# Weight pieces of 1 MB in eighteen ring places, logits without a wait for the last turned tile, and two small moves beside the first pair, in a two-layer MoE decoder trunk

## What is computed

```python
def reference(x, ...):
    h = x
    for i in range(2):
        xn = rms_norm(h, norm_mix[i])
        mix = sliding_window_attention(xn, ...) if i == 0 else gated_short_conv(xn, ...)
        h = h + mix
        h = h + hierarchical_moe(rms_norm(h, norm_ffn[i]), ...)
    return rms_norm(h, final_norm)

def hierarchical_moe(h, w_group, b_group, w_expert, b_expert, w_gate_up, w_down):
    group_probs = softmax(xt @ w_group + b_group)          # 4 groups, top 1
    exp_logits = xt @ w_expert + b_expert                  # 8 experts in a group, top 2
    ...
    def expert_block(xb, e):                               # 32 experts
        g, u = split(xb @ w_gate_up[e], 2)                 # w_gate_up[e]: 1024 x 1024
        return (silu(g) * u) @ w_down[e]                   # w_down[e]: 512 x 1024
```

## Time and profile before

| | us |
|---|---|
| three runs | 1341.44, 1341.86, 1343.41 |
| median | 1341.86 |
| the profiled execution's own time | 1341.31 |
| its span | 1339.6 |

### The profile page before, as it was taken

The page is one execution under the profiler, slowest core; times in us unless marked ns, Lnnn a source line. Parts: engine busy times, 40 slices in busy tenths (PEclk is TensorE's granted clock), DMA queues, the critical chain, the costliest instruction groups (busy, mean ns, idle before and its releaser), DMA issues.

```text
span 1339.6 us, 15996 instructions
## 1 busy us (share of the span) xinstructions
PE 1281.9 (96%) x6188; PEld 687.6 (51%) x6188; DVE 498.7 (37%) x1178; ACT 311.7 (23%) x622; POOL 148.9 (11%) x122
## 2 busy tenths in 40 slices
PE   7999999999999998989999999999999999999896
PEld 5777664444444433334588888744444444433342
DVE  5586342223222322224656662432223222322235
ACT  3267611111111111111443321211111111111103
POOL 4950120000000000000000002200001000000000
PEclk9999989999999999999999999899999999999999
DMA  9901569999999999999823336689999999999997
GB/s 347 342 8 60 255 259 419 429 427 428 429 427 429 428 428 426 428 427 426 257 88 105 103 142 267 250 347 427 427 428 428 427 428 428 429 426 428 426 428 296
DMA packets 68579, 462.53 MB, mean 345 GB/s; under 512 B 18020, under 2 KB 33406, under 8 KB 43956
## 3 DMA queue, kind: packets, MB, share of 16 engines
q1 hardware_dynamic: 63232, 452.87, 81.6%
q0 software_dynamic: 4800, 7.96, 1.6%
q10 hardware_dynamic: 500, 1.06, 0.2%
HBM read 443.40 MB, written 26.24 MB: 351 GB/s over the span
## 4 chain that ended last, share of the span: by engine, by line
PE 75%; DMA 21%; DVE 2%; ACT 0%; issue 0%; SPq 0%; POOLq 0%; DVEq 0%
PE ps L1170 22%; PE ps L962 20%; PE ps L1188 13%; DMA big<-in_moe_w_gate_up_dram 12%; PE ps L1145 8%; DMA small<-in_moe_w_gate_up_dram 6%; DMA big<-rows 2%; PE ps L1160 2%; PE ps L1179 1%; PE ps L926 1%; PE ps L1105 1%; PE ps L1271 1%; PE ps L1154 1%; PE ps L1044 1%; PE ps L1011 1%; PE ps L945 1%
## 5 line engine op out<-in xcount | busy, mean ns | idle before, releaser
L1170 PE MATMUL ps<-big,arena 128*64 128x512 f32 x976 | 218.2, 594 | 17.1 <-DMA big<-in_moe_w_gate_up_dram 15.6
L1685 DVE SCALAR_TENSOR_TENSOR gain<-ps,slot_root,arena 64x512 f32<-64x512 f32 x64 | 72.8, 1137 | 403.1 <-ACT arena L810 402.1
L617 POOL DMA_INDIRECT rows<-arena x60 | 59.0, 983 | 827.7 <-DVE arena L1713 827.7
L1170 PEld LDWEIGHTS ps<-big,arena 128*64 128x64 f32 x976 | 68.9, 137 | 158.4 <-issue 131.1
L810 ACT ACTIVATE arena<-ps,slot_root 64x512 f32<-64x512 f32 x64 | 43.7, 682 | 452.6 <-PE ps L1170 452.6
L1170 PE MATMUL ps<-small,arena 128*64 128x512 f32 x496 | 111.9, 593 | 5.1 <-DMA small<-in_moe_w_gate_up_dram 5.1
L962 PE MATMUL ps<-xt_parts,small_parts 128*128 128x512 f32 x288 | 110.6, 393 | 0.0
L962 PE MATMUL ps<-xr_parts,small_parts 128*128 128x512 f32 x272 | 105.9, 389 | 0.0
L1188 PE MATMUL ps<-big,arena 128*64 128x512 f32 x432 | 98.7, 598 | 1.5 <-DMA big<-in_moe_w_down_dram 1.5
L962 PE MATMUL ps<-xt_parts,big_parts 128*128 128x512 f32 x256 | 99.7, 389 | 0.0
L1170 PEld LDWEIGHTS ps<-small,arena 128*64 128x64 f32 x496 | 35.4, 137 | 77.0 <-issue 68.3
(11 more groups left out here) (218 smaller groups left out, 1687.7 us busy)
## 6 DMA issues: line engine op xcount, KB each, us to landing
big<-in_moe_w_gate_up_dram SPq DMA_DIRECT2D x61, 2048.0 KB, 27.9
small<-in_moe_w_gate_up_dram SPq DMA_DIRECT2D x31, 2048.0 KB, 28.6
big<-in_moe_w_down_dram SPq DMA_DIRECT2D x27, 2048.0 KB, 30.1
arena<-in_moe_w_gate_up_dram SPq DMA_DIRECT2D x16, 2048.0 KB, 30.1
small<-in_moe_w_down_dram SPq DMA_DIRECT2D x11, 2048.0 KB, 28.7
xt<-in_moe_w_gate_up_dram SPq DMA_DIRECT2D x10, 2048.0 KB, 25.4
h<-in_moe_w_gate_up_dram SPq DMA_DIRECT2D x10, 2048.0 KB, 24.7
xt<-in_moe_w_down_dram SPq DMA_DIRECT2D x10, 2048.0 KB, 31.8
```

Source lines behind the costliest of these rows:

```text
L617: nc.gpsimd.indirect_dma_start(out=rows_dram[l], out_offset=bass.IndirectOffsetOnAxis(ap=where[:, j:j + 1], axis=0), in_=S.y_rows[:, j, :] ...
L1170: mm = nc.tensor.matmul(ps[2 + j][half * BLOCK:(half + 1) * BLOCK, :], S.xg[:, k, j * BLOCK:(j + 1) * BLOCK], w[:, a, half * FF:(half + 1) ...
L1685: V.scalar_tensor_tensor(out=hid[BLOCK:P, j, :].rearrange("q (k p) -> q p k", p=P), in0=ps[2 + j][BLOCK:P, :].rearrange("q (p k) -> q p k" ...
```

## The change

Five edits:

1. A pair has twelve pieces of 1 MB (`PIECES = 12`, `PIECE = 2` rows to a partition), and the ring eighteen places, the halves of the old nine. The order of the bytes is the same. `gu_done` now counts quarters of a `w_gate_up`, `down_done` halves of a `w_down`. A run in HBM is 8 KB where it was 16 KB.
2. The semaphores of four loads of `x` and five others of the first stage are those of ring places 9 to 17, which are used later; the counts take this in.
3. `turn_tile` of the last tile ends without the wait for all copies in the two stages that come before logits; `logits` waits for its own tile alone.
4. For the first pair ACT copies one half of the gathered rows and DVE the other.
5. `last_gates` follows the first `take` and `find_rows`.

```diff
-    PIECES = 6
-    RING = 9
+    PIECES = 12
+    PIECE = 2
+    RING = 18
...
-        x_in = [sem(f"x_in{t}") for t in range(TT)]
...
+        FIRST_IN = RING // 2
+        x_in = ring_in[FIRST_IN:FIRST_IN + TT]
+        rel_in, query_in, w_o_in, kv_in, bo_in = ring_in[FIRST_IN + TT:]
...
+        ring = [[place[:, at:at + PIECE] for place in of_layer for at in range(0, FT, PIECE)] for of_layer in places]
...
                             before, used = divmod(n - RING, PIECES)
-                            if used < 4:
-                                sp.wait_ge(main[l].gu_done, 4 * before + used + 1)
+                            if used < 8:
+                                sp.wait_ge(main[l].gu_done, 8 * before + used + 1)
...
-                        if c < 4:
-                            w = w_gate_up[l, 2 * i + c // 2].rearrange("(p k) n -> p k n", p=P)[:, c % 2 * FT:(c % 2 + 1) * FT]
+                        if c < 8:
+                            w, part = w_gate_up[l, 2 * i + c // 4], c % 4
                         else:
-                            w = w_down[l, 2 * i + c - 4].rearrange("(p k) n -> p k n", p=P)
+                            w, part = w_down[l, 2 * i + (c - 8) // 2], c % 2
+                        w = w.rearrange("(p k) n -> p k n", p=P)[:, part * PIECE:(part + 1) * PIECE]
                         sp.dma_start(ring[l][n % RING], w).then_inc(ring_in[n % RING], 16)
...
             def experts(l):
                 S = main[l]
-                take_picked(S, 0)
+                take_picked(S, 0, (0,))
...
                     keep_busy(busy, 5)
+                    if i in (1, 3):
+                        return
                     pe.wait_ge(xt_even, TT * (i + 1))
                     pe.wait_ge(xt_odd, TT * (i + 1))
...
             def gate_up(S, j, part, w):
-                for a in range(FT):
-                    k = part * FT + a
+                for a in range(PIECE):
+                    k = part * PIECE + a
...
-            def down(S, n, j, w):
-                pe.wait_ge(S.hidT_ready, n + 1)
-                for k in range(FT):
+            def down(S, n, j, part, w):
+                if part == 0:
+                    pe.wait_ge(S.hidT_ready, n + 1)
+                for a in range(PIECE):
+                    k = part * PIECE + a
...
                 select(main[l], slice(0, 2))
+                dve.wait_ge(main[l].gathered, 1)
+                V.tensor_copy(picked[:, HALF:D], ps[1][:]).then_inc(main[l].rows_taken, 1)
                 dve.wait_ge(rank_ps, 2 * l + 2)
...
                 layer_gain[0] = gffn[:, l]
-                last_gates()
                 if l == 0:
                     dve.wait_ge(scales_in, 32)
                     dve.wait_ge(cleared, 16 * L)
                 take(S, 0)
                 find_rows(S, 0)
+                last_gates()
```

More of the change, by code:

```diff
@@ L536, in _ @@
                 if q < BIG_SLOTS:
[L537 removed]
+                    sp.wait_ge(main[0].gu_done, 4 * E)
                 else:
@@ L797, in router, with take_picked @@
                 nc.scalar.activation(rt[:, :, 20:21], rt[:, :, 20:21], ACT.Exp).then_inc(exp_ready, 1)
-            def take_picked(S, i):
+            def take_picked(S, i, halves_taken=(0, 1)):
                 act.wait_ge(S.gathered, i * 3 + 1)
-                for half in range(2):
+                for half in halves_taken:
                     nc.scalar.activation(picked[:, half * HALF:(half + 1) * HALF], ps[half][:], ACT.Copy)\
```

61 lines of the change are left out of this document (29 added, 32 removed).

## The result

The changed kernel takes 1349.08 us (median of 5 runs, 1348.28 to 1349.92) beside 1341.44 us of the kernel before in the same comparison: a ratio of 1.0057, 95% interval 1.0042 to 1.0072. It is 7.6 us slower. The forecast was 1346.6 us with a range of 1334 to 1350.5; case A came about, 2.5 us above its middle.

The account below looks back on a forecast made before the run. The prediction took the full transfer engines, streaming expert weights, as the bound. From the profiled 1341.31 us, -5.6 (moment) - 0.5 (tail) + 10.9 (rate) gave 1346.1, or 1346.6 for the median of runs; range 1334 to 1350.5.

Parts of the forecast that it names:

- case A: Weight stream: 8 KB packets have the rate of the line through other packet sizes; 1346.6 us, 1342.6 to 1351, chance 42%.
- The form of the sum: Each layer's experts: the moment the stream becomes continuous, plus bytes still to come over the rate, plus a fixed tail.
- (a): First expert matmuls: a ring place is free after half a piece, so the next load issues 1.75 us earlier per layer.
- (b): First pair's take: with last_gates behind it, DVE takes the first half sooner, 0.45 us a layer, 0.9 in all.
- (c): First pair's row copy on two engines: nothing gained, since PE's own order starts the turning.
- (d): Logits before the experts: matmuls start 0.65 and 0.9 us earlier, gaining 0.5 us in layer 0 and 0.7 in layer 1.
- its upper bound: Logits term: if the clock should not fall, or rise sooner, DVE's masks set the start, 1.8 us in each layer.
- the moment: Tenth load's issue, when the stream becomes continuous: 5.6 us earlier over both layers, between 4.2 and 8.0.
- The empty stretch takes all of it: Empty queue before the tenth load, 6 us in each layer: long enough to absorb the whole earlier moment.
- The rate: Expert weight stream: 8 KB packets go at 422.6 GB/s, 5.4 us later per layer, 10.9 in all.
- rival B: Weight stream: 16 KB rate is a ceiling 8 KB packets also reach, so only gains stand; 1335.8 us, chance 33%.
- The tail: Layer 0's end: PE may get to some of line 1247's matmuls sooner, 2 us at most; 0.5 us gain taken.

Follow-up runs that it names:

- half pieces alone: The changed kernel with the three small edits (logits, two-engine copy, last_gates) undone, keeping 1 MB pieces in eighteen places: 1352.49 us, ratio 1.0098 to the kernel before.
- the kernel of two loads: The kernel before with each 2 MB piece fetched by two 1 MB loads of 8 KB runs into the same nine places: 1351.31 us, ratio 1.0087.
- a single half place: Kernel before plus the three small edits, whole pieces, only each layer's tenth piece fetched as two 1 MB loads: 1335.12 us, ratio 0.9970 to the kernel before.
- the small edits: The kernel before with only the logits, two-engine copy and last_gates edits, pieces whole: 1335.24 us, ratio 0.9972; again 1335.75 us, 0.9976.
- the three kernels above: The kernel before with gate and up in 8 KB runs (ratio 1.0078), all pieces in 8 KB runs (1.0113), or gate and up in 4 KB runs (1.0182).

## Why the prediction was right, and where its sizes were not

**The form of the sum** held: a moment, plus the stream, plus a tail. The stream was full to the end, PE waited for the half pieces near the end, as it had for the whole ones, and the rows followed the weights. PE in layer 0, pair 14, where the earlier trace rows has pieces 4.92 us apart (these lines are from the changed kernel's timeline):

```profile
598.38 1.94 PE L1174 MATMUL ps<-big,arena 128*64 128x512 f32 x8 [0.35 <-DMA big<-in_moe_w_gate_up_dram]
600.87 1.94 PE L1174 MATMUL ps<-small,arena 128*64 128x512 f32 x8 [0.56 <-DMA small<-in_moe_w_gate_up_dram]
```

Half pieces come 2.5 us apart.

**(a) Half pieces, -1.75 a layer.** Measured -1.72 and -1.71 from the first matmuls to the issue. Against the kernel with 8 KB runs and whole places, though, issue to rows is 0.3 (half pieces alone) to 0.6 us (the changed kernel) longer, so 1.1 to 1.4 net, and less against the kernel of two loads. Not seen in the prediction; with a single half place 0.7 to 0.9 are left.

The prediction covered twice the loads with 0.33 us for each issue. That held for the first pairs, but not later: from 440 to 636 us 63 of 73 issues of a load of 1 MB take over 1.5 us, 2.1 in the middle and up to 6.6. Four of them in the changed kernel:

```profile
598.05 11.13 SPq L482 DMA_DIRECT2D big<-in_moe_w_gate_up_dram  x4
```

The kernel before has 0.33 us for each there, and so have the small edits; every kernel whose stream has 8 or 4 KB packets has long ones, with a median over the weight loads of that stretch of 2.1 us for 1 MB and of 4.6 to 5.2 us for 2 MB. Could this, and not the packet, be what slows the stream? No: in the changed kernel the stream has the same rate ahead of it, 421 GB/s with 0.33 us for every issue from 240 to 290 us, and in it, 421 from 440 to 600.

```profile
240.00:290.00 50.00, 50.00 (x249) 20.65 (x246) 13.54 (x34) 7.94 (x13) 3.89 (x4) 1.00 1.01 421
440.00:600.00 160.00, 148.02 (x700) 59.16 (x696) 37.47 (x87) 23.18 (x36) 10.27 (x11) 1.00 1.01 421
```

**(b), (c) Takes and gates, -0.45 and 0.** Measured 0.3 to 0.4 for both together in each layer.

**(d) Logits, -0.5 and -0.7.** At equal clock right in layer 0 (0.6) and short in layer 1 (1.1); beside the one profile of before mis-sized. In layer 1 the clock did not fall at all, so the stretch from turning to selection lost 3.2 us (13.28 to 10.12), of which 1.1 is the edit's. In layer 0 it lost 2.3 us (13.18 to 10.90), of which 0.6 is the edit's and the rest a shorter fall. The prediction had this as its upper bound ("If the clock should not fall, or rise sooner", 1.8 in each layer), with DVE's masks taking over as the limit, and that is the row at 864.77, waiting 1.16 for DVE. The step that failed was to move the matmuls under a clock that stays where one profile had it: whether and for how long it falls differs from one profile to the next. In all the moment came 9.5 us sooner, not 5.6, and 3.8 of the 9.5 are this difference between two profiles; at equal clock it is 5.7.

**"The empty stretch takes all of it"** held, and just. In layer 1 the moment came 5.2 us sooner, and of the 6 us next to nothing is left: the traffic there runs on at 422 and 299 GB/s. Any further gain ahead of the experts would find about one microsecond to fill in layer 1 and 2 us in layer 0.

**The rate, +5.4 a layer.** Mis-sized: +7.1 and +7.4. Two causes. The larger is the cost of a packet: the prediction laid one line through the 4 KB row (6 ns a packet) and one through the 1 KB row (9 ns) and took the middle. The kernel with the same packets in whole places lost 6.5 and 6.9 us, 9.3 and 9.9 ns for each of the 696, so the line through 1 KB was the better one and 421.5 GB/s the rate, not 422.6. The rest, 0.6 and 0.5, is what the half pieces lose in the stream, under (a).

A fixed part for each packet beside one for the bytes is what the three kernels above show: 428 GB/s with 16 KB, 421.5 with 8 KB, 1.5% less, and 409 with 4 KB, which is worked out above. So 428 GB/s is no ceiling that packets of 16 and 8 KB both reach, as rival B had it. Take 9 ns off the 612.5 ns of a 16 KB packet, and its bytes alone would go at 434 GB/s, an estimate from these two numbers.

**The tail, -0.5.** Wrong in sign: +2.07 at the end of layer 0. PE does end its last down product sooner, by 1.7 us against the first row tile. But the step that failed was what PE's 2.33 us of idle time were put down to: the prediction had PE wait for DVE's rest, so that 12 of the 32 matmuls could go ahead of it. PE was in its branch until 646.40, 0.13 us ahead of that rest, and could have run none of them. In the changed kernel the branch takes 1.2 us longer, and line 1254 runs with the clock at half for longer (6.40 where it was 5.53). Layer 1's end gave -0.08.

**The ends of the cases.** With the tail at 0.5 us the terms put case A between 1342.2 and 1350.2 and the low end of B at 1333.4, not the 1342.6, 1351 and 1332.3 written. Nothing hangs on it.

**The sum.** Forecast -5.6 - 0.5 + 10.9; measured -9.5 + 2.1 + 14.4, and 0.6 that lies ahead of every edit: +7.6. Both large terms were too small, by 3.9 and 3.5 us, in opposite directions, and nearly all of the 3.9 is the clock of two single profiles; that luck, and not the sizes, kept the forecast within 2.5 us.

The version that is faster than both kernels is the one without half pieces: the three small edits, 0.9972 and 0.9976 of the time before.

## What to carry to other kernels

Where a stream is full for hundreds of microseconds, what a load's shape costs is multiplied by all of its packets, and what an earlier start gives is had once. Half the size of a place won 1.7 us a layer here at the start, and packets of half the length cost 6.5 and 6.9 us (696 more on an engine, 9.3 and 9.9 ns each): look first whether the runs in HBM can keep their length. Before a finer ring, look for what the first freed place waits for, and then for the next one: with one place cut, the gap moved one load further, and 0.8 to 1.0 of the 1.7 us went back. Read a gain at a place where the clock falls against several profiles of the same order, not one. And where an engine is idle behind a jump in its program, look for the branch and its code before you count on the idle time: here it took 4.8 to 6.3 us in layer 0, and 12 matmuls that the prediction wanted to put there could not have run.

## What the hardware showed that was not expected

- A packet of this stream costs some 9 ns beside its bytes (8.9 to 10.4 ns at 8 and 4 KB over both layers, worked out above): 428 GB/s with 16 KB, 421.5 with 8 KB, about 409 with 4 KB. Twice the load instructions added nothing: 96 of 2 MB or 192 of 1 MB gave 450.2 and 449.6 us for the same stretch.
- A jump of PE over code that doesn't run took 4.8 to 6.3 us where a fetch of 16 KB of code fell inside it, in all fourteen profiles of layer 0, and 0.35 us in layer 1, where none did.
- SP's issue of a load of 1 MB in packets of 8 KB took 0.33 us behind the first pair and mostly 2.1 us late in a layer; with 16 KB packets a load of 2 MB kept its 0.33 us to the end.
- The granted clock differed in one and the same order of instructions: ahead of layer 1's experts it didn't fall at all, or to half for 3.4 or 6.8 us. Without an idle time of 0.90 us of PE ahead of the place it fell in none of seven profiles where it had in four of seven; in layer 0, with 0.17 us of idle time for 0.83, in six of seven where it had in four.

```profile
178.00:180.00 2.00, 2.00 (x8) 1.15 (x8) 1.25 (x11) 0.00 (x0) 0.00 (x0) 0.64 1.03 430
180.00:182.00 2.00, 2.00 (x4) 0.77 (x3) 1.83 (x15) 0.21 (x1) 0.00 (x0) 0.51 1.00 422
182.00:184.00 2.00, 2.00 (x6) 0.88 (x5) 1.83 (x15) 0.21 (x1) 0.00 (x0) 1.00 1.01 426
```

This is layer 0 of the changed kernel: four passes in the two microseconds at 0.51, six at 1.00, with PE busy the whole time in both.
- The part ahead of every edit differs too: the last turned tile of layer 0 starts between 172.94 and 174.82 us over the fourteen profiles. Single profiles are to be compared by stretches, not by their spans.
